# Recurrent gate products as four 64x64 tiles of TensorE, with the first unit's blocks set between projection groups

## The reference, cut to what matters

```python
def block_diag(x, w, b):                      # w: (16, 64, 64)
    xb = x.reshape(B, S, 16, 64)
    return (jnp.einsum('bsnc,ncd->bsnd', xb, w) + b).reshape(B, S, 1024)

def rglru(x, wa, ba, wi, bi, lam, reverse):
    r = sigmoid(block_diag(x, wa, ba)); i = sigmoid(block_diag(x, wi, bi))
    log_a = 8.0 * r * log_sigmoid(lam)
    a = exp(log_a); u = sqrt(-expm1(2.0 * log_a)) * (i * x)
    return associative_scan(linear_combine, (a, u), reverse=reverse)
```

## Time and profile before

| what | value |
|---|---|
| three runs | 1162.07, 1167.43, 1166.57 us |
| median | 1166.57 us |
| span of the profiled execution | 1161.2 us (the page gives no other time for it) |
| TensorE busy | 1081.6 us, 93% of the span |
| VectorE busy | 382.9 us, 33% |
| ScalarE busy | 234.2 us, 20% |
| DMA | 439.89 MB, mean 379 GB/s |
| mean granted TensorE clock | 0.994 |

### The profile page before, as it was taken

One profiled execution on the slowest core, in us unless ns is written; L12 is line 12 of the kernel. 1 busy time (PEld: TensorE's weight loads), 2 busy tenths in 40 slices (PEclk: granted clock), 3 DMA queues, 4 the chain that ended last, 5 costly groups with the idle time before them and its releaser, 6 DMA issues.

```text
span 1161.2 us, 13145 instructions
## 1 busy us (share of the span) xinstructions
PE 1081.6 (93%) x5391; PEld 502.8 (43%) x5391; DVE 382.9 (33%) x671; ACT 234.2 (20%) x371; POOL 0.2 (0%) x4
## 2 busy tenths in 40 slices
PE   5998999989999999999998989898989898989997
PEld 5998789823333333333333323332333233323332
DVE  6996798532322222222121212121211212121122
ACT  5388843100111111111111111111110101010112
POOL 0000000000000000000000000000000000000000
PEclk9999999989999999999999999999999999999999
DMA  8543146998999999999999999999999999999996
GB/s 351 186 171 145 73 160 278 418 400 333 429 397 425 431 425 429 428 428 429 428 429 428 430 428 427 430 428 428 430 428 428 429 428 430 428 427 429 429 428 248
DMA packets 32618, 439.89 MB, mean 379 GB/s; under 512 B 3760, under 2 KB 3888, under 8 KB 5712
## 3 DMA queue, kind: packets, MB, share of 16 engines
q1 hardware_dynamic: 32112, 438.53, 89.9%
q10 hardware_dynamic: 480, 0.99, 0.2%
HBM read 438.46 MB, written 1.05 MB: 378 GB/s over the span
## 4 chain that ended last, share of the span: by engine, by line
PE 61%; DMA 33%; DVE 4%; ACT 1%; issue 1%; SPq 0%; DVEq 0%
DMA slot<-in_w_gu_dram 27%; PE ps L1333 25%; PE ps L1037 12%; PE ps L1342 10%; DMA slot<-in_w_down_dram 6%; PE ps L1305 4%; PE ps L1286 3%; PE ps L1300 1%; PE ps L1387 1%; DVE slot_r L627 1%; PE ps L1092 1%; PE ps L1135 1%; PE ps L1264 1%; PE ps L1156 1%; PE ps L1365 0%
## 5 line engine op out<-in xcount | busy, mean ns | idle before, releaser
L1333 PE MATMUL ps<-slot,lru 128*64 128x512 f32 x880 | 198.9, 595 | 21.0 <-DMA slot<-in_w_gu_dram 20.7
L1342 PE MATMUL ps<-slot,lru 128*64 128x512 f32 x896 | 203.3, 596 | 14.8 <-DMA slot<-in_w_down_dram 14.3
L1333 PE MATMUL ps<-slot,qT 128*64 128x512 f32 x880 | 202.1, 601 | 14.4 <-DMA slot<-in_w_gu_dram 12.9
L1333 PEld LDWEIGHTS ps<-slot,lru 128*64 128x64 f32 x880 | 62.7, 137 | 147.6 <-issue 113.5
L1333 PEld LDWEIGHTS ps<-slot,qT 128*64 128x64 f32 x880 | 62.5, 137 | 147.1 <-issue 134.9
L1342 PEld LDWEIGHTS ps<-slot,lru 128*64 128x64 f32 x896 | 62.3, 137 | 135.4 <-issue 117.1
L558 ACT ACTIVATE lru<-ps 128x512 f32<-128x512 f32 x32 | 19.1, 598 | 419.7 <-PE ps L1333 419.7
L993 DVE TENSOR_TENSOR lru<-ps,cst 128x1024 f32<-128x1024 f32 x32 | 39.2, 1225 | 141.5 <-PE ps L1387 141.5
L970 DVE TENSOR_SCALAR lru<-sq,x_sb,small 128x64 f32<-128x64 f32 x66 | 17.7, 312 | 188.1 <-PE ps L1286 188.1
L1037 PE MATMUL ps<-wide_r,slot_r 128*128 128x256 f32 x492 | 66.2, 286 | 0.2 <-DVE slot_r L627 0.2
L1305 PE MATMUL ps<-lru 128*128 128x512 f32 x136 | 63.9, 593 | 0.9 <-DVE lru L1017 0.9
(11 more groups left out here) (212 smaller groups left out, 905.1 us busy)
## 6 DMA issues: line engine op xcount, KB each, us to landing
slot<-in_w_gu_dram SPq DMA_DIRECT2D x110, 2048.0 KB, 34.9
slot<-in_w_down_dram SPq DMA_DIRECT2D x55, 2048.0 KB, 33.2
wide<-in_w_gu_dram SPq DMA_DIRECT2D x15, 2048.0 KB, 34.8
slot<-in_pre_dram SPq DMA_DIRECT2D x14, 2048.0 KB, 8.3
wide<-in_w_down_dram SPq DMA_DIRECT2D x8, 2048.0 KB, 35.3
slot<-in_w_lru_dram SPq DMA_DIRECT2D x2, 1024.0 KB, 13.3
wide<-in_w_gu_dram SPq DMA_DIRECT2D x2, 1024.0 KB, 14.8
late<-in_w_gu_dram SPq DMA_DIRECT2D x1, 2048.0 KB, 16.8
```

Of the source, the lines that this page charges most:

```text
L1333: ins = nc.tensor.matmul(ps[64 * side:64 * side + 64, 4 + b, :], xgT[i % 2][:, k, :], rows[r][:, o:o + BANK], start=(k == 0), stop=(k == K ...
L1342: ins = nc.tensor.matmul(ps[64 * side:64 * side + 64, bank, :], actT[(i - 1) % 2][:, k, :], w[:, r, side * BANK:(side + 1) * BANK], start= ...
```

## The change

The four matrices of a block no longer go through TensorE as 128x128 matrices half full of zeros. Each is taken as two 64x64 products, one for each 64 channels, so a block has eight products. Those of the forward direction (m = 0, 1) read `xc` as before and lie on the diagonal of the array (rows 0 to 63 with columns 0 to 63, and 64 to 127 with 64 to 127). Those of the backward direction (m = 2, 3) read `xc_other`, a copy of `xc` in which the two halves of the partitions have changed places, with weights that are swapped likewise, and lie off the diagonal. So four products that follow each other use four different quarters of the array. The copy is made by SyncE's queue (two DMAs for each unit) in the buffer `gA`, and each unit's weights come in three DMAs in place of one. One semaphore step stands for a whole block: ScalarE waits for all of a block's products, and TensorE for the reads of the whole block before.

The order changes too. Unit 0's blocks 1, 2 and 3 stand behind groups 8, 9 and 10. Unit 1's blocks stand in steps 17, 19, 20 and 21. ScalarE takes the square root for the queries and keys before unit 0's last block, and the decay parts of unit 1 move to steps 21, 22 and 23.

```diff
+        xc_other = gA
+        UNIT1_AT = [17, 19, 20, 21]
 @block.sync
+            def load_lru_weights(u):
+                w_sb = ring[LOWS][:, KD * TOK:]
+                sp.dma_start(w_sb[:, 0:1024], w_lru[u][:, 0:1024]).then_inc(lruw_in, 16)
+                for r in range(2):
+                    sp.dma_start(w_sb[64 * r:64 * r + 64, 1024:], w_lru[u][64 - 64 * r:128 - 64 * r, 1024:]
+                                 ).then_inc(lruw_in, 16)
-                    sp.dma_start(ring[LOWS][:, KD * TOK:], w_lru[0]).then_inc(lruw_in, 16)
+                    load_lru_weights(0)
+                if c in (4, 6):
+                    u = 0 if c == 4 else 1
+                    sp.wait_ge(conv_ok, 4 * u + 4)
+                    for r in range(2):
+                        sp.dma_start(xc_other[64 * r:64 * r + 64, 4 * u:4 * u + 4, :],
+                                     xc[64 - 64 * r:128 - 64 * r, 4 * u:4 * u + 4, :]).then_inc(xc_moved[u], 16)
                 if c == 6:
                     sp.wait_ge(gate_ps, 16)
-                    sp.dma_start(ring[LOWS][:, KD * TOK:], w_lru[1]).then_inc(lruw_in, 16)
+                    load_lru_weights(1)
 @block.scalar
                 for c in blocks:
+                    act.wait_ge(gate_ps, 16 * u + 4 * c + 4)
                     for m in range(4):
-                        n = 16 * u + 4 * c + m
-                        act.wait_ge(gate_ps, n // 2 * 2 + 2)
...
-            lru_gates(0, range(4))
+            lru_gates(0, range(3))
             act.wait_ge(qk_inv, 1)
             nc.scalar.activation(qk_rstd, qk_rstd, ACT.Sqrt).then_inc(qk_rs, 1)
+            lru_gates(0, [3])
             split_high(6)
...
-                if 17 <= i < 21:
-                    lru_gates(1, [i - 17])
+                if i in UNIT1_AT:
+                    lru_gates(1, [UNIT1_AT.index(i)])
...
-                if 20 <= i < 23:
-                    lru_decay(1, i - 20)
+                if 21 <= i < 24:
+                    lru_decay(1, i - 21)
 @block.tensor
+                pe.wait_ge(xc_moved[u], 32)
                 for c in [4 * u + b for b in blocks]:
                     pe.wait_ge(conv_ok, c + 1)
-                    for m in range(4):
-                        n = 4 * c + m
-                        if n >= 4:
-                            pe.wait_ge(gate_read, n // 2 * 2 - 2)
-                        nc.tensor.matmul(half(6 + (n % 4) // 2, n % 2), lru_w_sb[:, m, c % 4, :], xc[:, c, :],
-                                         start=True, stop=True).then_inc(gate_ps, 1)
+                    if c >= 1:
+                        pe.wait_ge(gate_read, 4 * c)
+                    for k in range(2):
+                        for m, src in ((k, xc), (2 + k, xc_other)):
+                            for r in range(2):
+                                rows, o = slice(64 * r, 64 * r + 64), 64 * r if m < 2 else 64 - 64 * r
+                                ins = nc.tensor.matmul(half(6 + m // 2, k)[o:o + 64, :], lru_w_sb[rows, m, c % 4, o:o + 64],
+                                                       src[rows, c, :], start=True, stop=True)
+                    ins.then_inc(gate_ps, 4)
...
-            lru_gate_products(0, range(4))
+            lru_gate_products(0, [0])
             for i in range(8, 14):
                 group(i)
+                if i < 11:
+                    lru_gate_products(0, [i - 7])
...
-                if 17 <= i < 21:
-                    lru_gate_products(1, [i - 17])
+                if i in UNIT1_AT:
+                    lru_gate_products(1, [UNIT1_AT.index(i)])
```

More of the change, by code:

```diff
@@ L182, in encoder_layer @@
         lruw_in = sem("lru_weights_in")
+        xc_moved = [sem(f"xc_halves_moved{u}") for u in range(2)]
         split_hi, split_lo = sem("chunk_high"), sem("chunk_low")
@@ L413, in lru_gates @@
                 for c in blocks:
+                    act.wait_ge(gate_ps, 16 * u + 4 * c + 4)
                     for m in range(4):
-                        n = 16 * u + 4 * c + m
-                        act.wait_ge(gate_ps, n // 2 * 2 + 2)
                         dst = (lruR if m % 2 == 0 else lruI)[:, (m // 2 * 4 + c) * TOK:(m // 2 * 4 + c + 1) * TOK]
                         b = C_LB + m * 8 + 4 * u + c
-                        nc.scalar.activation(dst, half(6 + (n % 4) // 2, n % 2), ACT.Tanh, scale=0.5,
+                        nc.scalar.activation(dst, half(6 + m // 2, m % 2), ACT.Tanh, scale=0.5,
                                              bias=cst[:, b:b + 1]).then_inc(gate_read, 1)
@@ L1084, in lru_gate_products @@
             def lru_gate_products(u, blocks):
-                pe.wait_ge(lruw_in, 16 * (u + 1))
+                pe.wait_ge(lruw_in, 48 * (u + 1))
+                pe.wait_ge(xc_moved[u], 32)
                 for c in [4 * u + b for b in blocks]:
                     pe.wait_ge(conv_ok, c + 1)
-                    for m in range(4):
-                        n = 4 * c + m
-                        if n >= 4:
-                            pe.wait_ge(gate_read, n // 2 * 2 - 2)
-                        nc.tensor.matmul(half(6 + (n % 4) // 2, n % 2), lru_w_sb[:, m, c % 4, :], xc[:, c, :],
-                                         start=True, stop=True).then_inc(gate_ps, 1)
+                    if c >= 1:
[7 more added lines that the diff above has]
+                    ins.then_inc(gate_ps, 4)
             pe.wait_ge(sq_in, 16)
```

## The result

After the change the kernel takes 1167.21 us (median, 1165.21 to 1169.75), before it 1164.44 us (1161.60 to 1167.43), 20 runs each: ratio 1.0028, interval 1.0019 to 1.0037, so 2.8 us more, within what I had called no change and in the direction forecast. The profiled execution has a span of 1164.3 us against 1161.2, +3.1.

The account below looks back on a forecast made before the run. TensorE up to head 6's scores, then VectorE's list, set the mixer's end; the weight stream bounds the expert part. Span 1161.2 + 2.8 = 1164.0; median 1166.6 + 2.8 = 1169.4 us, mostly 1166 to 1172.

Parts of the forecast that it names:

- TensorE's own time: Mixer, TensorE: a block of products takes 1.22 us against 1.73; eight blocks save 4.1 us, step 19 0.2 more.
- The rival of turn-taking: Row halves of TensorE's array run in turn: a round 0.432 us, a block 2.1, total 1174; chance 0.11.
- Unit 0: Mixer, unit 0: group 8 starts 4.0 us early, but group 12 waits for ScalarE, near 78.1 against 75.1.
- The clock, a rival: New idle stretches on TensorE make its clock fall once, for some 7 us: +3.4, 1173; chance 0.07.
- the forecast's case: Mixer's waits for ScalarE outweigh TensorE's saving: branch products 2.8 us late, 1169.4 us; chance 0.66.
- Unit 1: Mixer, unit 1: group 20 starts at 107.7 against 110.54, 2.8 us early; group 22 about 1.1 early, at 121.3.
- The decay's last part: Mixer, step 23: ScalarE ends it at 138.3, VectorE waits, `head_max(6)` starts at 141.3 instead of 138.24, +3.1 us.
- TensorE's whole saving arrives: Mixer: no wait on ScalarE at group 12, none at the decay; the lead grows to some 7 us, 1160; chance 0.04.
- DMAs at nothing: Mixer: the new copies and weight loads come in time and add no time to the sum.

Follow-up runs that it names:

- the first experiment: The kernel before with unit 1's three decay parts one step later, in steps 21, 22, 23: 1168.8 us, ratio 1.0038 to the kernel before.
- the filler: The kernel after with unread matmuls added, 24 before group 12 and 20 before head 6's transposes: 1167.46 us, ratio 1.0026 to the kernel before.
- The best version: The kernel after with unit 0's blocks 0 and 1 ahead of group 8 and the last decay part in step 22: 1158.27 us, ratio 0.9952.

## Why the prediction was right, step by step

**TensorE's own time: right.** Rounds of four are 0.215 us apart (forecast 0.216, taken from column pairs, as no row showed row halves together), a block is 1.21 (forecast 1.22). The rival of turn-taking, which wanted 0.43, is false: here r = 0 and r = 1 write different partitions of one PSUM bank, and still the four records of a round run together (those of the block at 62.63 all by 62.65) and the rounds are 0.215 us apart. That a matmul's issue costs nothing extra was an estimate which no row bore; measured, four rounds by 0.215 are 0.86 us, 0.054 for each of the 16 records, as the sum had it.

**Unit 0: right.** Group 8 at 59.56 (59.5), group 11 at 71.84 (71.8), group 12 at 78.34 (near 78.1), by the chain named: tanh's table again, tanh, split, reads. The pair of blocks in front of group 8 took group 12's start back by 3.9 us, and `head_max(6)` came 3.9 us earlier.

**The clock, a rival: in part true beside the forecast.** I had put 0.07 on a fall of some 7 us at the new gaps. One of 3.4 us came at group 12 and cost 4.43 - 2.88 = 1.55 us. It explains most of what the mixer lost beyond the forecast: +4.57 at the branch products, less 1.55, is 3.0, for 2.8. I had set it as a case of its own; it was a surcharge on the forecast's case, and the kernel before pays one too, in some executions. The median clock of the two is the same, 0.994, so their medians should carry about as much of it; that their difference is 2.8, the forecast to the tenth, is in part luck. The rival also read the earlier trace rows as TensorE waiting: those 2 us have it busy for all of 2.00; the low stretch there began at 233.3, in a wait of 1.01 us that ended at 233.57.

**Unit 1: right in kind, late by 2 us.** Group 20 started at 110.90, not 107.7. 1.55 of the 3.2 is the clock; the rest is a wait of 1.62 us for `split_low(7)` on VectorE, which I had not followed. By group 22 (123.36 for 121.3) all but 0.5 of this second part was gone, since the waits for ScalarE that I had put there then fell away. With that wait removed it came back at the next tanh: the limit is ScalarE's serial list, so the miss cost little.

**The decay's last part: right, and the step that decides.** ScalarE ran it from 136.15 to 140.19 (forecast 134.2 to 138.3, the 1.9 us being again clock and split), `lru_square(1)` waited 5.74 us (forecast some 5), `head_max(6)` followed 2.94 us behind its start (forecast 3.0). Four pairs of runs bear it: between the two reads of scores it costs 4.0 us moved later alone, and gives 3.7 us moved back in the kernel after; the order alone shows the same wait; and on top of the earlier blocks of unit 0 it gives 9.57 - 5.84 again (129.68 to 139.25 for 129.32 to 135.16).

**TensorE's whole saving arrives: false** for this kernel, and the reasons named held, for with both waits cut short 4.7 us of it, counted from block 0, did arrive at the branch products. The rival had some 7.

**DMAs at nothing: right.** The four copies to `hn` were issued at 44.25 and 56.22 us and landed some 6.8 us after issue by the median, and no product waited for one.

## What to carry to other kernels

The faster products on the engine that leads (0.51 us a block) bought only an earlier meeting with the next engine's serial list, and the kernel took 2.8 us more: follow that list, instruction by instruction, to the first read that is itself on time only by luck. Moving a call one step later in a hand-written order can put it behind reads that hang on the leading engine; here one such call, the decay's last part, cost 4 us and moving it back regained the whole loss. Last, in the mixer of these profiles the stretches at 0.50 began within waits of TensorE of 1.6 to 4.4 us or up to 1.7 us behind them, and the same wait had one in some executions only. In the router seven of the twelve began in or up to 1.3 us behind waits of 0.85 to 1.01 us, and five with TensorE at work and no wait over 0.1 us in the 10 us before. Count such a stretch as a possible surcharge on every case, for the kernel before as well, compare medians over many runs, not two profiles, and look at the mean clock of every run beside its time.

## What the runs showed of the hardware that I had not expected

The same idle stretch is followed by a fall of the granted clock in one execution and not in another. The 3.16 us before the block at 101.75 left it at 1.00 in the profile before, while it was 0.50 for 10.2 us, from 100.6, in that of the first experiment; 2.73 us before group 8 left it at 1.00 in the kernel after, while the kernel with the earlier decay has it at 0.50 from 61.5; 1.62 us before group 20 had no fall behind it in the kernel after and had one, at 109.6, with the filler. Between the first block and the end of the weight stream the low stretches in these twelve profiles were about 3.4, 6.8 or 10.2 us long. What decides between the cases, none of the runs shows.

The best version's gain by medians (6.2 us, expected 4) is larger than its 4.7 us between block 0 and the branch products. Its executions have the higher mean clock (median 0.9965 for 0.994), and fewer low stretches fit the rest; no run isolates it.

The profiles differ ahead of the change as well. The 32 matmuls that start near 15.3 us took 4.10 us in the profiles of before and after, 5.92 in that of the best version and 6.37 in that of the tiles in the old order, while the granted clock of these windows is 1.00 in all four; the first block then starts 1.2 to 1.8 us later. The cause stays open. Whoever compares start times of two profiles has to count from a common point ahead of the change.
